# Expert biases of a mixture layer as products 32 rows deep in four row groups, with the expert's rows picked on ScalarE

## The reference, cut to what matters

```python
xb = hf[tok]
g = xb @ w_gate[e] + b_gate[e]
u = xb @ w_up[e] + b_up[e]
g = jnp.minimum(g, SWIGLU_LIMIT)
u = jnp.clip(u, -SWIGLU_LIMIT, SWIGLU_LIMIT)
act = (u + 1.0) * (g * jax.nn.sigmoid(g * SWIGLU_ALPHA))
y = act @ w_down[e] + b_down[e]
return y * gt[:, None].astype(y.dtype)
```

## Time and profile before

| | |
|---|---|
| median of three runs | 2264.97 us |
| the profiled execution | 2263.67 us |
| its span, first to last instruction | 2261.8 us |
| TensorE busy, products | 2183.6 us, 97% |
| VectorE busy | 652.2 us, 29% |
| ScalarE busy | 563.0 us, 25% |
| POOL busy | 461.3 us, 20% |
| granted clock of TensorE, mean | 0.986 |
| DMA, mean over the span | 221 GB/s |
| products of expert weights with input rows, line L1493 | 969.0 us |
| bias products of gate and up, line L1487, records | 188 |

### The profile page before, as it was taken

How to read it: one execution, slowest core, us unless ns; L and a number is a source line. 1 busy time by engine, 2 the same in 40 slices (tenths; PEclk the granted TensorE clock), 3 DMA queues, 4 the chain that set the end, 5 groups by cost and what they waited for, 6 DMA issues and landing times.

```text
span 2261.8 us, 30785 instructions
## 1 busy us (share of the span) xinstructions
PE 2183.6 (97%) x10323; PEld 1010.8 (45%) x10324; DVE 652.2 (29%) x1919; ACT 563.0 (25%) x1156; POOL 461.3 (20%) x490
## 2 busy tenths in 40 slices
PE   8999899997899999999999899999999999999997
PEld 4444477543444444344434334434443444444443
DVE  2100599354322222121122223212212121322223
ACT  2000488311221222221122222212112121222223
POOL 1014011214121122211221212221122212122222
PEclk9999999998899999999999999999999999999998
DMA  6100300224558967938878795794889958677775
GB/s 264 41 0 0 149 1 1 87 107 152 193 190 312 351 218 241 359 115 327 303 254 318 259 344 186 241 370 120 312 324 363 373 206 295 250 250 258 247 266 187
DMA packets 148184, 499.68 MB, mean 221 GB/s; under 512 B 10137, under 2 KB 34350, under 8 KB 146574
## 3 DMA queue, kind: packets, MB, share of 16 engines
q1 hardware_dynamic: 112480, 443.80, 50.8%
q0 software_dynamic: 33792, 50.35, 10.8%
q10 hardware_dynamic: 1874, 5.02, 0.6%
HBM read 460.84 MB, written 42.50 MB: 223 GB/s over the span
## 4 chain that ended last, share of the span: by engine, by line
PE 93%; DMA 3%; DVE 1%; POOL 1%; issue 1%; ACT 1%; ACTq 0%; DVEq 0%; SPq 0%; POOLq 0%
PE psum L1493 41%; PE psum L1529 14%; PE psum L1251 10%; PE psum L1306 5%; PE psum L1540 4%; PE psum L1324 3%; PE psum L1295 3%; PE psum L1415 2%; DMA weights<-in_w_down 2%; PE psum L1501 2%; PE psum L1487 2%; PE psum L1475 1%; PE psum L1552 1%; PE psum L1564 1%; PE psum L1333 1%
## 5 line engine op out<-in xcount | busy, mean ns | idle before, releaser
L1493 PE MATMUL psum<-weights,work 128*128 128x512 f32 (+2 forms) x3008 | 969.0, 594 | 0.0
L1493 PEld LDWEIGHTS psum<-weights,work 128*128 128x128 f32 (+2 forms) x3008 | 365.6, 159 | 449.8 <-issue 443.8
L605 POOL DMA_INDIRECT residual_rows<-work x184 | 286.6, 1558 | 447.3 <-ACT work L805 400.9
L1529 PE MATMUL psum<-weights,work 128*128 128x512 f32 x768 | 337.5, 592 | 0.0
L1061 DVE TENSOR_REDUCE work<-psum 128x8 f32 x47 | 8.6, 184 | 795.0 <-PE psum L1429 795.0
L565 POOL DMA_INDIRECT work<-normed_rows,work x48 | 49.3, 1028 | 861.4 <-DVE work L1048 802.9
L1251 PE MATMUL psum<-weights 128*128 128x512 f32 x512 | 220.9, 593 | 1.3 <-DVE weights L877 1.3
L1529 PEld LDWEIGHTS psum<-weights,work 128*128 128x128 f32 x768 | 144.0, 190 | 164.3 <-issue 160.7
L777 ACT ACTIVATE work<-psum 128x256 f32<-128x256 f32 x188 | 71.9, 383 | 385.8 <-PE psum L1493 362.1
L764 ACT ACTIVATE work<-psum 128x512 f32<-128x512 f32 x96 | 57.6, 600 | 435.0 <-PE psum L1415 433.3
L1139 DVE TENSOR_SCALAR work<-psum 128x256 f32<-128x256 f32 x188 | 79.6, 424 | 259.8 <-ACT work L777 253.2
(11 more groups left out here) (214 smaller groups left out, 1678.5 us busy)
## 6 DMA issues: line engine op xcount, KB each, us to landing
weights<-in_w_gate SPq DMA_DIRECT2D x64, 2048.0 KB
weights<-in_w_up SPq DMA_DIRECT2D x64, 2048.0 KB
weights<-in_w_down SPq DMA_DIRECT2D x64, 2048.0 KB, 10.6
weights<-in_w_in SPq DMA_DIRECT2D x8, 1024.0 KB, 15.5
residual_rows<-x SPq DMA_DIRECT2D x9, 512.0 KB, 3.8
normed_rows<-work ACTq DMA_DIRECT2D x9, 512.0 KB, 3.9
x<-in_x SPq DMA_DIRECT2D x8, 512.0 KB, 9.4
bias_rows_repeated<-bias_rows SPq DMA_DIRECT2D x4, 1024.0 KB, 9.4
```

Source lines behind the costliest of these rows:

```text
L605: pl.indirect_dma_start(acc_d[:, :], bass.IndirectOffsetOnAxis(dest[:, b:b + 1], 0), yrow[:, b * BLK:(b + 1) * BLK], None, compute_op=ALU. ...
L1493: mm = pe.matmul(out.rearrange("p (m n) -> p m n", m=2), xT[:, k, lo:lo + cols], wgu[:, :, k, blk * BLK:(blk + 1) * BLK], start=False, sto ...
L1529: mm = pe.matmul(bank(4 + h), actT[:, k, :], wdn[:, k, h * HALF:(h + 1) * HALF], start=False, stop=(k == DT - 1))
```

## The change

The split biases are laid out again. `brow_all` has four sets of eight experts each, side by side in the columns. In a set partition 32 b + 3 i + part holds, for the i-th of the eight experts, block b of 256 columns of the gate and up biases and half b % 2 of the down bias; the other eight partitions of each 32 are zero. POOL clears `brow_all`, and SyncE fills it with 96 transfers from SBUF to SBUF (`bias_rows`, 24 for a set), between the stores of the residual rows. For each item ScalarE multiplies the expert's set by a column of `of_place`, which is one in the three rows of the expert in each 32 and zero elsewhere, and writes `brow`, 128 x 1024 in bfloat16. It does so after the last `move_hidden` and ahead of `yrow`. VectorE's `choose` and its register load go. The bias products have a matrix of ones as stationary operand and are 32 rows deep; those for block b use partitions 32 b to 32 b + 31, thus row group b of TensorE. All products for the gate and up biases of an item stand at its head, after one wait for the hidden rows of all four units of the item before. The two products (four in 32-column groups) of the down bias take row groups 0 and 1 (0 to 3). In kind 32 TensorE increments a semaphore that nobody waits for, ahead of the bias products in both places.

```diff
-        chosen = small(64).bitcast(BF16)
-        bgu = biasp[0:3 * EXPERTS, 0:2 * D].rearrange("p (m n) -> p m n", m=2)
-        bdn = biasp[0:3 * EXPERTS, 2 * D:3 * D]
+        bsrc = biasp[:, 0:2 * D].rearrange("p (m b n) -> p m b n", m=2, b=UNIT)
+        dsrc = biasp[:, 2 * D:3 * D].rearrange("p (h n) -> p h n", h=2)
+        brow_all = Z[:, 12288:12288 + ROW_SETS * HALF]
+        brow_sets = brow_all.bitcast(BF16)
+        brow = Z[:, 16896:16896 + HALF].bitcast(BF16)
+        brow_gu = brow[:, 0:HALF].rearrange("p (m n) -> p m n", m=2)
+        brow_dn = brow[:, HALF:]
...
+            def bias_rows(n):
+                for b in range(UNIT):
+                    for part in range(3):
+                        to = slice(32 * b + part, 32 * b + part + 3 * ROW_SET - 2, 3)
+                        of = slice(EXPERTS * part + ROW_SET * n, EXPERTS * part + ROW_SET * n + ROW_SET)
+                        at = 2 * n * HALF
+                        sp.dma_start(brow_sets[to, at:at + HALF].rearrange("p (m n) -> p m n", m=2),
+                                     bsrc[of, :, b, :]).then_inc(s_browin, 16)
+                        sp.dma_start(brow_sets[to, at + HALF:at + 2 * HALF], dsrc[of, b % 2, :]).then_inc(s_browin, 16)
...
             for i in range(TT + 1):
                 sp.wait_ge(s_x1, 2 * min(i, TT - 1) + 2)
                 sp.dma_start(acc_rows[i * P:(i + 1) * P, :], xv[:, i % TT, :]).then_inc(s_accin, 16)
+                if i == 4:
+                    sp.wait_ge(s_biasp, 1)
+                    sp.wait_ge(s_cleared, 1)
+                    bias_rows(0)
+                if 4 <= i < 4 + ROW_SETS - 1:
+                    bias_rows(i - 3)
...
+                if i == 4:
+                    pl.wait_ge(s_biasp, 1)
+                    pl.memset(brow_all, 0.0).then_inc(s_cleared, 1)
                 if i >= 4:
                     gate_parts(i - 4)
...
+            def choose(e, of_set):
+                act.activation(brow, brow_sets[:, of_set], ACT.Copy, scale=of_place[:, e]).then_inc(s_chosen, 1)
+
+            act.wait_ge(s_browin, 16 * 24 * ROW_SETS)
+            choose(slice(0, 1), slice(0, 2 * HALF))
...
                 with act.If(j < n_items - 1):
+                    follower = act.value_load(items[0:1, bass.ds(j + 1, 1)], min_val=0, max_val=EXPERTS - 1)
...
                     move_hidden(j, 3)
+                    act.wait_ge(s_biased, j + 1)
+                    choose(bass.ds(follower, 1), bass.ds(follower // ROW_SET * (2 * HALF), 2 * HALF))
                     act.wait_ge(s_dest, j + 2)
...
-                    e1 = dve.value_load(items[0:1, bass.ds(j + 1, 1)], min_val=0, max_val=EXPERTS - 1)
...
-                    dve.wait_ge(s_biased, j + 1)
-                    choose(bass.ds(e1, 1))
...
+            def rows_of(b):
+                return slice(32 * b, 32 * b + 32)
...
+                def bias(b):
+                    if tokens == 32:
+                        for c in (0, 2, 1, 3):
+                            out = PS[32 * c:32 * c + 32, b * HALF:(b + 1) * HALF].rearrange("p (m n) -> p m n", m=2)[:, :, 0:P]
+                            blk, first = divmod(b * HALF + c * P, BLK)
+                            pe.matmul(out, onesb[rows_of(blk), 0:32], brow_gu[rows_of(blk), :, first:first + P],
+                                      start=True, stop=False)
+                        return
+                    cols = P if tokens == 128 else 64 if b < 2 else 32
+                    for c in range(P // cols):
+                        blk = b if cols == P else 2 * c + b if cols == 64 else c
+                        out = PS[c * cols:(c + 1) * cols, b * HALF:(b + 1) * HALF].rearrange("p (m n) -> p m n", m=2)
+                        pe.matmul(out, onesb[rows_of(blk), 0:cols], brow_gu[rows_of(blk), :, :], start=True, stop=False)
...
                 def down_bias():
                     pe.wait_ge(s_yr, UNIT * j + UNIT)
+                    if tokens == 32:
+                        pe.sem_inc(s_pbegin, 1)
                     if tokens == 128:
                         for h in range(2):
-                            mm = pe.matmul(bank(4 + h), chosen[0:3 * EXPERTS, :], bdn[:, h * HALF:(h + 1) * HALF],
-                                           start=True, stop=False)
+                            mm = pe.matmul(bank(4 + h), onesb[rows_of(h), :], brow_dn[rows_of(h), :], start=True, stop=False)
...
                         for h in range(4):
-                            mm = pe.matmul(PS[32 * h:32 * h + 32, at:at + BLK], chosen[0:3 * EXPERTS, 0:32],
-                                           bdn[:, h * BLK:(h + 1) * BLK], start=True, stop=False)
+                            b = h // 2 + 2 * (h % 2)
+                            mm = pe.matmul(PS[32 * h:32 * h + 32, at:at + BLK], onesb[rows_of(b), 0:32],
+                                           brow_dn[rows_of(b), h % 2 * BLK:h % 2 * BLK + BLK], start=True, stop=False)
...
                 pe.wait_ge(s_chosen, j + 1)
                 pe.wait_ge(s_xT, 2 * j + 1)
                 pe.wait_ge(s_wk[0], 32 * e + 32)
+                pe.wait_ge(s_hid, UNIT * j + UNIT)
+                if tokens == 32:
+                    pe.sem_inc(s_pbegin, 1)
                 for b in range(units):
-                    pe.wait_ge(s_hid, UNIT * j + b + 1)
+                    bias(b)
+                for b in range(units):
                     mm = gate_up(b, range(4))
```

More of the change, by code:

```diff
@@ L51 @@
 TABLE = MAX_ITEMS + 3
+ROW_SET = 8
+ROW_SETS = EXPERTS // ROW_SET
 EPS = 1e-5
@@ L188, in encoder_kernel @@
         dgate = small(4)
-        tables = small(24 + EXPERTS)
+        tables = small(24 + 2 * EXPERTS)
         place, away, of_row = tables[:, 0:12], tables[:, 12:24], tables[:, 24:24 + EXPERTS]
+        of_place = tables[:, 24 + EXPERTS:24 + 2 * EXPERTS]
         items = small(3 * TABLE)[0:1, :].bitcast(I32)
@@ L319, in encoder_kernel @@
         s_chosen = sem("expert_chosen")
+        s_pbegin = sem("small_products_begun")
+        s_cleared = sem("bias_rows_cleared")
+        s_browin = sem("bias_rows_of_units_in")
         s_biased = sem("down_bias_done")
@@ L403, in _ @@
             sp.wait_ge(s_o, UNITS)
-            sp.dma_start(tables[:, :], t["tables"][:, 0:24 + EXPERTS]).then_inc(s_tabin, 16)
-            sp.dma_start(spreadf, t["tables"][:, 24 + EXPERTS:]).then_inc(s_tabin, 16)
+            sp.dma_start(tables[:, :], t["tables"][:, 0:24 + 2 * EXPERTS]).then_inc(s_tabin, 16)
+            sp.dma_start(spreadf, t["tables"][:, 24 + 2 * EXPERTS:]).then_inc(s_tabin, 16)
             sp.dma_start(gain2, t["norm2"].partition_broadcast(P)).then_inc(s_gain2, 16)
@@ L1069, in places @@
                 dve.wait_ge(s_found, n + 1)
-            def choose(e):
-                dve.tensor_scalar(chosen[0:3 * EXPERTS, :], onesb[0:3 * EXPERTS, :],
-                                  of_row[0:3 * EXPERTS, e], None, ALU.mult).then_inc(s_chosen, 1)
             compare(pick0)
@@ L1455, in _ @@
             n_items = pe.value_load(total[0:1, 0:1], min_val=EXPERTS, max_val=MAX_ITEMS)
+            def rows_of(b):
+                return slice(32 * b, 32 * b + 32)
             def item(j, e, e2, tokens):
-                def gate_up_32(b, ks):
[L1466 to L1470, removed]
+                def bias(b):
[11 more added lines that the diff above has]
+                        pe.matmul(out, onesb[rows_of(blk), 0:cols], brow_gu[rows_of(blk), :, :], start=True, stop=False)
+                def gate_up_32(b, ks):
                     for k in ks:
@@ L1482, in gate_up @@
                         (64 if b else 0, 32, 4)
[L1483 to L1486, removed]
-                            pe.matmul(out, chosen[0:3 * EXPERTS, 0:cols], bgu[:, :, blk * BLK:(blk + 1) * BLK],
-                                      start=True, stop=False)
                     for k in ks:
@@ L1505, in down_bias @@
                     pe.wait_ge(s_yr, UNIT * j + UNIT)
+                    if tokens == 32:
+                        pe.sem_inc(s_pbegin, 1)
                     if tokens == 128:
                         for h in range(2):
-                            mm = pe.matmul(bank(4 + h), chosen[0:3 * EXPERTS, :], bdn[:, h * HALF:(h + 1) * HALF],
-                                           start=True, stop=False)
+                            mm = pe.matmul(bank(4 + h), onesb[rows_of(h), :], brow_dn[rows_of(h), :], start=True, stop=False)
                     if tokens in (64, 96):
                         for h in range(2):
-                            mm = pe.matmul(PS[64 * h:64 * h + 64, 4 * HALF:5 * HALF], chosen[0:3 * EXPERTS, 0:64],
-                                           bdn[:, h * HALF:(h + 1) * HALF], start=True, stop=False)
+                            mm = pe.matmul(PS[64 * h:64 * h + 64, 4 * HALF:5 * HALF], onesb[rows_of(h), 0:64],
+                                           brow_dn[rows_of(h), :], start=True, stop=False)
                     if tokens in (32, 96):
@@ L1733 @@
```

(3 more changed lines are left out.)

2 lines of the change are left out of this document (removed).

## The result

The changed kernel takes 2272.64 us, the median of seven runs (2270.04 to 2273.61), against 2262.96 of the kernel before beside it (2258.67 to 2265.85, seven runs): ratio 1.0048, 95% interval 1.0037 to 1.006. It is slower by 9.7 us, where 2262.2 had been forecast in a range up to 2272. The profiled execution took 2272.64 us with a span of 2270.7, 8.9 longer than before, at a mean granted clock of 0.981 (0.986 before).

A forecast was written before the change was run, and what follows sets the result against it. TensorE, issuing back to back over the expert loop, was taken as the bound. 4.4 us saved there less 1.6 for ScalarE's pick gave 2.8, so 2264.97 became 2262.2 us, range 2254 to 2272.

The forecast's parts named there:

- the head of the expert stage: Before the expert loop: clearing and 96 SyncE transfers at 0.47 us end at 550, ahead of w_up's issue at 552.51; cost 0.
- rival D: SyncE comes late: beyond 0.66 us a transfer w_up is late for the first item; at 0.9, 2287 us; chance 0.06.
- POOL's clearing: Ahead of the transfers: POOL clears 2048 columns after the last split at 500.5, estimated at 2 us, until 502.5.
- The head of kind 128: Gate and up bias products of 128 items: 0.46 us for 0.88; saves 0.42, or 0.33 after another 128 item.
- The down bias of kind 128: Down bias products in 128 items: 0.53 us against 0.44, loses 0.10 an item.
- Kinds 64 and 96: Bias products in 15 items of these kinds: lose some 0.06 us an item, 0.9 in all.
- Kind 32: Eight items: 1.0 us lost in head and down bias, 0.6 for semaphore increments, 1.6 for the pick.
- the pick: ScalarE's 1024-element copy after 32 items: 1.06 us, late by about 0.27 in six items, 1.6 lost (0 to 3).
- The sum: Whole kernel: 4.4 us saved on TensorE less 1.6 for the pick, 2.8 saved, 2262.2 us.
- E: Rival: row groups run one after the other, 43 us lost with pick and increments, 2308 us; chance 0.06.
- B's far end: Rival that TensorE's switches cost little (2256); wholly free, 128 items save 0.83 us each, reaching 2240; chance 0.20 for B.
- C's point: Rival: ScalarE's pick sets item starts after short ones; a 2 us copy loses 8 us in all, 2269; chance 0.12.

The follow-up runs named there:

- head alone: Changed kernel with only gate and up biases in row groups, down bias as before, 48 transfers, pick of 512 elements: 2253.61 us, ratio 0.9962.
- transfers alone: Kernel before plus the clearing, the 96 transfers and a ScalarE wait for them, products unchanged: 2277.99 us, ratio 1.0068.
- switch at each unit: Changed kernel with each unit's bias product directly ahead of that unit's weight products again: 2313.0 us, one run.
- one turn earlier: Changed kernel with splitting, clearing and the 96 transfers each one turn of the router's loop earlier: 2263.19 us, ratio 1.0005 to the kernel before.

## Why the prediction was wrong

**The step that failed** is the head of the expert stage: "A small one costs 0.42, the two beside each other in one row 0.47 each with the gap", "hidden by 2 us", "Cost of the stage: 0". The 0.42 was the load of the up biases of all experts from HBM, and the prediction took eight rows from SBUF for no dearer. They hold SyncE 0.73 and 0.66, every 0.73 us. The sum itself was built right: its 505 + 96 x 0.73 is 575.1, and `w_up` was issued at 574.97. The slack behind it was overrated as well: 16 us were allowed for `w_up`'s first half, where 11.2 covered the delay (14.2 by a load of 8.2 us, less some 3 by which the late load is slower). With the right price and the prediction's own allowance, 552.5 + 16, the first head would have been 6.6 us late (575.1 less 568.5); it was 11.3, and the first item lost 2.4 more. This was rival D; it was given 0.06 although its point, 0.66 us a transfer, lay only a factor of 1.4 above the spacing of 0.47 that was read from the one row at hand.

**POOL's clearing** was estimated at 2 us up to 502.5; it took 1.80 and the first transfer started at 501.91. Held.

**The head of kind 128.** Forecast 0.46 for 0.88 (the terms that are listed add up to 0.45). Measured 0.33 held, where 0.40 to 0.46 was the sign that was named (0.39 in the first item of the kind and 0.54 in two others), and 0.08 more behind it (32 records start in 13.84 us, 719.54 to 733.38, where 4 x 3.44 is 13.76): 0.41 in most items. Items with another width behind them became 0.37 shorter (forecast 0.32), those with another of kind 128 behind them 0.28 (forecast 0.23), in sum 7.7 for 6.9. The head alone gives the separate figure, 0.45 an item.

**The down bias of kind 128** was to lose 0.10; it lost 0.07 to 0.09. Held.

**Kinds 64 and 96** were to lose 0.06 an item, and lost 0.07 and 0.06. The sum held; in kind 96 its parts did not, since there the head loses 0.08 and the down bias gains 0.03 (from the kernel with the head alone), for 0.03 and 0.02 lost in the forecast.

**Kind 32** was to lose 3.2 us over eight items, with 1.6 of them for the pick. The waits for the pick came as forecast: five, of 1.9 us in all, up to 0.4 each. The timeline of the changed kernel, ScalarE and TensorE at the end of such an item, answers to the earlier trace rows:

```profile
877.46 0.42 ACT L810 ACTIVATE work<-psum 128x256 f32<-128x256 f32 x1
877.72 1.18 ACT L814 ACTIVATE work<-work 128x1024 bf16 x1
879.23 0.40 PE L1509 MATMUL psum<-work 32*128 32x512 bf16 x4 [0.37 <-ACT work L814]
```

The pick ends at 878.90, and the head starts 0.33 behind it; the wait is 0.37 for a forecast of 0.27, and the copy took 1.15 for 1.06. By the table the seven items lost 1.7, no more than the waits, so that switches and increments would have cost nothing. That is in part an accident of the two traces: the one of the kernel before has VectorE's long distance (1.1) and the changed kernel's has the short one (0.46). Held against the kernel with the transfers alone, which has the short one too, the five items without a wait for weights are 0.48 longer, for 0.12 of switches and 0.27 of the wait in the forecast. The wait is 0.38 of it: from the start of the last down products to the next head it is 3.16, for 2.78 with the head alone. The down bias is 0.03 to 0.06. The head of eight products holds TensorE 0.23, no more than two times the 0.12 of the earlier trace rows, and comes to 0.03; further on the engine stands still for 0.37 ahead of the first hidden rows anyway, which covers it. So the switches cost a little less than forecast and the wait a little more; for the increments nothing is left that could be told. These rows answer to the earlier trace rows:

```profile
864.74 0.30 PE L1502 MATMUL psum<-work 32*32 32x256 bf16 x8
864.97 3.66 PE L1516 MATMUL psum<-weights,work 128*32 128x256 f32 x64
...
873.88 0.30 PE L1536 MATMUL psum<-ident,work 128*128 128x128 f32 x1 [0.37 <-issue]
...
874.59 0.29 PE L1554 MATMUL psum<-work 32*32 32x256 bf16 x4
874.80 1.07 PE L1601 MATMUL psum<-weights,work 128*32 128x256 f32 x16
```

**The sum.** Forecast for the loop, -2.8 us; measured -5.2, of which 0.8 came from kind 128 and 1.5 from kind 32; 1.0 of this 1.5 is the accident of VectorE's distance in five items, and luck. The 13.7 us of the head and the first item, forecast at 0, turned it round. E fell with the four products starting side by side; B's far end with the 0.51 of a switch at each unit; C's point with a copy of 1.15 us, near the 1.06 assumed, not 2.

The versions without the late `w_up` still start their first head 1.7 us later than before (576.60 to 576.70) and issue `w_up` 1.9 to 2.3 later. Where this comes from was not found. In the head-alone kernel 1.0 of it is there ahead of the router's stage (a transpose near the attention's end, L1341 before, at 434.97 for 433.97), and over all traces of this study that transpose starts anywhere from 433.15 to 436.21; each is one execution.

## What to carry to other kernels

Many small transfers are paid for by the queue that issues them, one after the other, so price them by a row of the same form (same source and target memory, and the same rows and pieces: from HBM alone the price was 0.30 or 0.65) and count up what stands behind them on that queue: the next big load. When the nearest row lies within a factor of two of the price at which a hidden stage comes out, that stage is no longer a zero with a chance of 0.06 against it. And take a change apart: here the head alone gains 8 us, while the down bias, with its half of the transfers and of the pick, gives back all of it and more. A short item that waits for another engine can differ by 0.2 us between two traces of the same code, so hold it against more than one.

## What the runs showed of the hardware

- A transfer from SBUF to SBUF holds SyncE 0.59 to 0.73 us if it is one of many, for 8 KB as for 32 KB; from HBM 0.30 in one form and 0.65 in others; a store of 96 rows to HBM 0.32.
- The same 2 MB of `w_up` take 8.2 us from issue to landing at 554.45 (head alone), 12.0 at 561.82 (one turn earlier, with the gather behind it) and 11.0 at 574.97 (changed kernel, with `w_down` 2.5 behind it).
- Four bf16 products 32 rows deep with 512 columns in four row groups hold TensorE 0.33 us with the way out, where a single one holds it 0.32. The Trainium skill, TensorE: Matmul & The Clock Gate (Part 3, measured speedup), gives 3.07x for four, by which they would take 0.06 longer than one (an estimate from that figure); they took 0.01 longer, and the measurement decides.
- A bf16 copy on ScalarE takes 1.15 us for 1024 columns and 0.72 for 512, with a scale by partition. TensorE's product that waits for it starts 0.33 after its end (878.90 to 879.23).
